# The first two halves of the cached values: from behind the last projection tile to behind the landings of the tiles before it

## The reference

```python
mod = silu(c) @ w_ada + b_ada                       # six adaLN vectors, w_ada 1024 x 6144
h = normalize(x) * (1 + scale1) + shift1
qa, ka, va, qb, kb, vb, ga, gb = split(h @ w_in)    # w_in 1024 x 5888
# samples: each of 8 rows attends to 2048 cached keys and values, 8 heads x 64,
# which lie in 16 pages of 128 rows, found through page_table
kp = pages_k[pt].reshape(past, n_h, dh)
vp = pages_v[pt].reshape(past, n_h, dh)
# softmax over the chosen blocks and the own block, times the values
mix = (sigmoid(ga) * (oa @ w_proj_a) + sigmoid(gb) * (ob @ w_proj_b)) @ w_out
x = LN(alpha * x + gate1 * mix)
# then a mixture of 32 experts (top 2 within the best of 4 groups), and a second LN
```

## Time and profile before

| What | Value |
|---|---|
| time, median of 3 runs | 1096.56 us (1094.95 to 1098.03) |
| time of the profiled execution | 1094.32 us |
| its span, first to last instruction | 1092.2 us |
| busy share of the span: PE, DVE, ACT, POOL | 78%, 32%, 17%, 11% |
| mean granted clock of PE, as a share of full speed | 0.90 |
| DMA: moved, mean rate | 396.30 MB, 363 GB/s |
| moved for SP's queue (q1), POOL's (q0), ACT's (q10) | 296.97, 85.90, 12.93 MB |

### The profile page before, as it was taken

How to read it: one execution, slowest core, us unless ns; L and a number is a source line. 1 busy time by engine, 2 the same in 40 slices (tenths; PEclk the granted TensorE clock), 3 DMA queues, 4 the chain that set the end, 5 groups by cost and what they waited for, 6 DMA issues and landing times.

```text
span 1092.2 us, 11668 instructions
## 1 busy us (share of the span) xinstructions
PE 847.7 (78%) x4564; PEld 465.0 (43%) x4564; DVE 344.8 (32%) x520; ACT 182.7 (17%) x429; POOL 115.6 (11%) x116
## 2 busy tenths in 40 slices
PE   6599898989979999992618888777877777877840
PEld 5484676468864454871513323222222222322210
DVE  2048998793243321327411100000000000000018
ACT  2311223222221110003302111101011111111110
POOL 1212211110012112000010000000000000000020
PEclk9799999999998885996658999999999999999975
DMA  9986999587999999999983999999999999999931
GB/s 313 399 316 245 401 408 400 201 323 282 355 359 429 426 393 350 381 365 354 373 328 156 426 425 425 423 426 428 426 426 424 425 427 424 426 427 422 419 113 45
DMA packets 70084, 396.30 MB, mean 363 GB/s; under 512 B 6418, under 2 KB 13094, under 8 KB 47847
## 3 DMA queue, kind: packets, MB, share of 16 engines
q1 hardware_dynamic: 50928, 296.97, 68.2%
q0 software_dynamic: 12016, 85.90, 19.6%
q10 hardware_dynamic: 7104, 12.93, 3.4%
HBM read 387.89 MB, written 58.10 MB: 408 GB/s over the span
## 4 chain that ended last, share of the span: by engine, by line
PE 44%; DMA 37%; DVE 13%; issue 3%; ACT 1%; SPq 1%; ACTq 0%; POOL 0%; POOLq 0%; DVEq 0%
DMA ring<-in_w_exp_up_dram 28%; PE bank L801 12%; PE bank L436 10%; DVE ring L1220 3%; DMA ring<-in_cache_v_pages_dram,pidx 3%; DVE S L1224 3%; PE bank L716 3%; PE bank L446 3%; DMA ring<-in_w_in_dram 2%; PE bank L633 2%; PE bank L703 1%; DMA ring<-in_cache_k_pages_dram,pidx 1%; PE bank L819 1%; PE bank L523 1%; PE bank L462 1%
## 5 line engine op out<-in xcount | busy, mean ns | idle before, releaser
L801 PE MATMUL bank<-ring,hT 128*64 128x512 f32 x1024 | 243.6, 631 | 43.7 <-DMA ring<-in_w_exp_up_dram 41.2
L801 PEld LDWEIGHTS bank<-ring,hT 128*64 128x64 f32 x1024 | 89.7, 144 | 196.2 <-issue 196.2
L1601 DVE TENSOR_TENSOR hT<-hT,bank 128x256 f32<-128x256 f32 x32 | 19.3, 603 | 415.4 <-ACT hT L1144 415.4
L436 PE MATMUL bank<-hT,ring 128*128 128x264 f32 x576 | 140.9, 403 | 5.8 <-DMA ring<-in_w_in_dram 5.8
L819 PE MATMUL bank<-ring,hT 128*64 128x512 f32 x512 | 118.6, 604 | 19.5 <-DVE hT L1604 19.5
L436 PEld LDWEIGHTS bank<-hT,ring 128*128 128x128 f32 x576 | 112.1, 198 | 27.5 <-issue 7.8
L1220 DVE TENSOR_TENSOR ring<-ring,qbc 128x4096 f32<-128x4096 f32 x16 | 70.7, 4417 | 43.1 <-ACTq L846 41.2
L1743 POOL DMA_INDIRECT expert_rows<-work,ridx x32 | 31.1, 971 | 470.4 <-ACT work L838 351.4
L838 ACT ACTIVATE work<-bank 128x512 f32<-128x512 f32 (+5 forms) x83 | 36.6, 451 | 221.9 <-PE bank L819 145.2
L819 PEld LDWEIGHTS bank<-ring,hT 128*64 128x64 f32 x512 | 40.9, 138 | 76.6 <-issue 76.6
L1224 DVE TENSOR_REDUCE S<-ring 128x64 f32<-128x4096 f32 x16 | 70.6, 4414 | 0.3
(11 more groups left out here) (303 smaller groups left out, 783.1 us busy)
## 6 DMA issues: line engine op xcount, KB each, us to landing
ring<-in_w_exp_up_dram SPq DMA_DIRECT2D x32, 2048.0 KB, 22.0
ring<-in_w_exp_down_dram SPq DMA_DIRECT2D x32, 2048.0 KB, 21.8
ring<-in_w_exp_gate_dram SPq DMA_DIRECT2D x32, 2048.0 KB, 17.5
ring<-in_w_ada_dram SPq DMA_DIRECT2D x12, 2048.0 KB, 13.9
out_dram<-in_state_dil_kv_dram SPq DMA_DIRECT2D x6, 4064.0 KB
ring<-in_w_in_dram SPq DMA_DIRECT2D x11, 2048.0 KB, 21.1
out_dram<-in_state_dil_kv_dram ACTq DMA_DIRECT2D x16, 508.0 KB, 7.7
out_dram<-in_state_dil_kv_dram SPq DMA_DIRECT2D x8, 992.0 KB
```

The lines of the kernel that those rows point to most:

```text
L436: i = mm(bk[:, 0:NT], w[:, k, j * P:(j + 1) * P], hT3[:, k, :], start=(k == 0), stop=(k == KC - 1))
L801: i = mm(side(2, half).rearrange("p (m n) -> p m n", m=2), xT[s][:, k, :], w[:, :, k, half * 256:(half + 1) * 256], start=(k == 0), stop=( ...
```

## The change

The first value half waits for the landing of ("ada", 10), and the second for that of ("win", 10); before, both waited for ("win", 11). The waits for the reduced keys stay, and so do the slots, the sizes and all that follows.

```diff
             for hh in range(2):
                 pool.wait_ge(s_kred, 2 * NB - 1 + hh)
-                if hh == 0:
-                    pool.wait_ge(w_full[slot_of(("win", 11))], ring_use["win", 11][2])
+                last = (("ada", 10), ("win", 10))[hh]
+                pool.wait_ge(w_full[slot_of(last)], ring_use[last][2])
                 page_half(v_pages, 0, hh, VSLOT[hh], v_full[hh])
             filled(pool, last_use[("win", 11)])
             page_half(v_pages, 1, 0, VSLOT[2], v_full[2])
```

## The result

The change took 1102.01 us in the median (1097.12 to 1107.01, 20 runs) against 1097.31 for the kernel before (1093.81 to 1100.19, 20 runs): a ratio of 1.0041, interval 1.0029 to 1.0053, so it is slower by 3.2 to 5.8 us. Forecast were 1098.6 us, +2.0 on a kernel before whose median was then 1096.56, and no change as the likeliest outcome (0.53). The size is more than twice the +2.0 of the sum, and by the prediction's own yardstick of 3.3 us it counts as slower, to which the prediction gave 0.30.

The account below looks back on a forecast made before the run. PE (44%) and DMA (37%) were taken to bound the kernel, with changes up to the cached values carried to its end. Terms 4.0 + 0 + 1.6 - 3.6 = +2.0 us gave 1098.6 us, 8-in-10 range 1093.0 to 1102.5.

Parts of the forecast that it names:

- ("win", 10) late, PE pauses 4.0 us: Projection stage: the first half delays this tile by 5.0 us against 1.0 us of slack, so PE waits 4.0 us.
- The estimate from a DMA ceiling: For ("win", 10): a 435 GB/s fabric ceiling leaves 90 GB/s to spare, giving 3.9 us of delay, 2.9 us of waiting.
- ("win", 11) in time: Last projection tile: lands at 314.7 us, PE wants it at 314.3 or 315.9; taken as 0, at most 1.5 us.
- The clock, 1.6 us: Just behind PE's pause in the projection stage: 16 matmuls at a lower clock take 1.6 us longer.
- First to third term: Projection stage: 4.0 us pause for ("win", 10), 0 for ("win", 11), 1.6 us for the clock; 5.6 us later.
- The value stage, -3.6 us: w_proj_a fits into the DMA hole before the third half, so PE's three waits for value halves go: -3.6 us.
- a stretch of lower clock in the value stage that comes or goes with the waits: Sign of being wrong: an effect in the value stage that no term holds, possibly worth 3 us either way.
- The rest one to one: From the value stage to the kernel's end: everything moves by the same 2.0 us, with no cover on the way.
- the fourth term: Value stage: PE's three waits for value halves go, -3.6 us, bounds 0 and -3.6.
- the rival that ends slower: Value stage: w_proj_a is issued later, the hole holds nothing and the waits stay; +5.6 us, 1102.2 us, chance 0.23.

Follow-up runs that it names:

- (a): Measured stretch, not a run: from SP's issue of ("ada", 11) to its issue of w_proj_a; 20.59 us before, 25.70 with the change in the first traces.
- (b): Measured stretch, not a run: from the first value matmul to the first of the dilated output; 81.91 us before, 79.26 with the change in the first traces.
- (c): Measured stretch, not a run: from the first dilated-output matmul to the first output projection; 22.44 us before, 21.80 with the change in the first traces.
- (d): Measured stretch, not a run: from the first output projection to the first store of the listed tokens; 111.90 us before, 112.20 with the change, first traces.
- (e): Measured stretch, not a run: the list's round trip, first store of the listed tokens to first use on PE; 23.85 us before, 27.11 changed, first traces.

## Why the prediction was right, and where it was off

*("win", 10) late, PE pauses 4.0 us.* Right, with 3.35, 3.33, 4.34 and 3.74 us in four traces. The mechanism is shown: the pause comes with the first half alone and goes when the copies are taken out of the stretch or issued earlier. The price that I took, a key half beside an earlier tile, 5.0 us, was measured as 22.4 - 18.1 = 4.3 to 23.4 - 18.1 = 5.3. The estimate from a DMA ceiling, 2.9 us of waiting, which I weighed and put aside, was too low in every trace. But my reason against it, that the engines' time is used up at 345 GB/s, was only half right: with the half among them the full engines moved 409 GB/s. What the half cost is nearer to its own engine time, 28.4% of 17.3 us, or 4.9 us. That "each half adds about 5 us", as a later expectation had it, was too simple as well: two halves in one queue cost the tile the same. The Trainium skill, page "DMA: Bandwidth & Descriptors", section "Queues, rings and completion order", says that each engine goes round between the queues that have work; by that rule a longer queue takes no more turns, and the trace agrees (22.9 against 22.4 us).

*("win", 11) in time.* Right by 1.5 us in the change. The slack was no safe margin: one tile later, the same half made ("win", 11) 9.4 us late and not 5.0, as the delayed copies met it. I had counted only the half's own bytes.

*The clock, 1.6 us.* Right: 5.51 - 3.83 = 1.7 us behind the pause. First to third term together were 5.6 in the sum, and (a) measures 5.4.

*The value stage, -3.6 us.* The first half of the term was right: w_proj_a lands in 8.0 us (and w_proj_b, which the term left out, in 5.3 us instead of 28.9), and the waits for halves shrink to 0.9, 0.6 and 0.2 us in the three whole traces. The step from there to -3.6 us was not. It took the waits of one trace as the gain, with PE's own work of a fixed length, and put the clock in this stage at nothing. A trace of before with one wait of 0.4 us has the same (b), because its matmuls lose 12.3 us at the lower clock instead of 9.1. The prediction had named this as a sign of being wrong, "a stretch of lower clock in the value stage that comes or goes with the waits", and it is there. (b) gives back 2.6 us: in the means of four, PE's idle time falls from 4.5 to 2.1 us, and the loss to the clock stays (9.9 and 9.8). Why the change, with as few waits as the second trace of before, loses 2 to 3 us less to the clock than it does, stays open. Part of it lies at the start of the stage, where the second 3.2 us have a granted clock of 1.00 in all four traces of the change, and of 0.73 to 0.80 in those of before.

*The rest one to one.* Nearly: +0.5 us in (c) and (d) together, most of it from one trace of the change (23.69 and 112.79). The sum of the measured parts is 5.4 - 2.6 + 0.1 + 0.4 = +3.4 us (with +0.05 between (a) and (b)) where the forecast had +2.0, and 3.4 lies inside the measured 3.2 to 5.8. The step that was mis-sized most is the fourth term, by 1.0 us.

*What stays open.* The median moved by 4.7 us, 1.3 more than the parts. The traces can't place this: their spans differ by 7.6 us in the mean of four, 3.4 in the parts, 0.9 in (e), 0.9 behind it, and 2.3 ahead of the edit, for the change issues ("ada", 10) at 273.4 us in the mean and before at 271.1 (the other kernels at 269.2 to 272.7). Whether that is chance of a few traces was not settled; the change with its copies earlier carries the same edit and loses nothing, so the edit as such is not what costs. That the time fell inside the range is in part luck: the range's upper end came from the rival that ends slower, 1102.2, whose mechanism did not occur, for w_proj_a did go into the hole.

## What to carry to other kernels

Moving a bulk transfer to an earlier time is free only where the engines' share is below full, and the share tells that, not the GB/s: here the engines were full at 345 GB/s, and at 409 with the half among them. The tile with the least slack between landing and use pays, here 1.0 us of slack against some 5 of delay. Transfers that nobody waits for (state copies) take their part of full engines beside the tile; issuing them earlier took the whole loss away. A wait that disappears is worth what it lasted only if PE's clock stays: here 3.5 us of waits less came with matmuls that took 3.5 us longer. A difference of two traces is read between two points of the same stage: here 4.4 of 11.2 us lay ahead of the edit.

## What the runs showed that I had not expected

The late state copies, off every list of causes in the prediction, hold the list's round trip: 12.5 us without the last 14 of them (7.93 MB by the two pages) against 23.9 to 27.2 with them, and the kernel 1.07% faster (0.83 to 1.31%), with those rows left unwritten. A kernel that makes these copies at another time, for which DMA's idle stretch just behind the list would be one place (1 GB/s from 573 to 590 us in the first trace of before), was not tried.
